# 64 slots for each expert in 32 blocks of two, gathers that leave out empty slots, and the sixth expert's weights loaded during the router

## What is computed

```
h2 = rms_norm(x, norm2_g).reshape(b * s, d)
g_sel = argmax(h2 @ w_rg + b_rg)              # one of 8 groups
top_v, top_i = lax.top_k(e_logits[g_sel], 2)  # 2 of its 8 experts
gate = p_group[:, None] * softmax(top_v)
hid = silu(xb @ w_gate_e[e]) * (xb @ w_up_e[e])
y = hid @ w_down_e[e]                         # for each expert e, its tokens xb
out = x + sum over a token's two experts of gate * y
```

## Time and profile before

| | |
|---|---|
| median of 3 runs | 2459.86 us (2456.59 to 2461.51) |
| profiled execution, its own time | 2460.95 us |
| its span in the profile | 2459.1 us |
| PE busy | 2084.4 us (85%) |
| DVE, ACT, POOL busy | 972.0, 683.7, 169.6 us |
| granted TensorE clock, mean | 0.93 of full speed |
| HBM read and written | 366.62 and 20.48 MB |
| loads of `in_wexp` | 66 of 2048 KB and 66 of 1024 KB |

### The profile page before, as it was taken

The page is one execution under the profiler, slowest core; times in us unless marked ns, Lnnn a source line. Parts: engine busy times, 40 slices in busy tenths (PEclk is TensorE's granted clock), DMA queues, the critical chain, the costliest instruction groups (busy, mean ns, idle before and its releaser), DMA issues.

```text
span 2459.1 us, 22973 instructions
## 1 busy us (share of the span) xinstructions
PE 2084.4 (85%) x9596; PEld 1442.3 (59%) x9596; DVE 972.0 (40%) x1472; ACT 683.7 (28%) x1076; POOL 169.6 (7%) x234
## 2 busy tenths in 40 slices
PE   6999778997999998999998999999946767777752
PEld 5887556887888787777777756666841222222211
DVE  3246443434666524577766255542250000000002
ACT  4233332324444314544444224431110000000000
POOL 1000000002000001010011021100021000000000
PEclk9999888998999999999999999999977888888876
DMA  6432110232322323111210221111276999999934
GB/s 183 137 124 82 43 52 35 103 137 95 103 87 102 137 89 130 69 56 69 73 56 35 99 80 39 48 52 69 112 291 228 425 425 421 411 419 419 418 122 163
DMA packets 51238, 383.34 MB, mean 156 GB/s; under 512 B 7904, under 2 KB 8176, under 8 KB 17984
## 3 DMA queue, kind: packets, MB, share of 16 engines
q1 hardware_dynamic: 38016, 341.33, 35.6%
q0 software_dynamic: 12544, 39.40, 5.1%
q10 hardware_dynamic: 576, 1.16, 0.2%
HBM read 366.62 MB, written 20.48 MB: 157 GB/s over the span
## 4 chain that ended last, share of the span: by engine, by line
PE 70%; DMA 13%; DVE 9%; ACT 4%; issue 2%; POOL 2%; SPq 0%; POOLq 0%; ACTq 0%
PE PS L481 15%; PE PS L482 15%; PE PS L483 15%; DMA AR<-in_wexp 11%; PE PS L958 6%; PE PS L834 4%; PE PS L980 2%; PE PS L528 2%; DVE AR L1174 1%; PE PS L893 1%; DVE rf L990 1%; PE PS L863 1%; ACT rf L1703 1%; DVE AR L1297 1%; DVE AR L1283 1%
## 5 line engine op out<-in xcount | busy, mean ns | idle before, releaser
L481 PE MATMUL PS<-rf,rf 128*128 128x512 f32 (+1 forms) x1896 | 724.2, 382 | 15.2 <-DVE rf L990 8.3
L482 PE MATMUL PS<-rf,rf 128*128 128x512 f32 (+1 forms) x1896 | 712.0, 376 | 0.0
L483 PE MATMUL PS<-rf,rf 128*128 128x512 f32 (+1 forms) x1896 | 711.5, 375 | 0.0
L990 DVE TENSOR_TENSOR rf<-AR,rf 128x1024 fp32r<-128x1024 f32 (+1 forms) x210 | 268.9, 1285 | 437.2 <-ACT rf L1703 437.0
L481 PEld LDWEIGHTS PS<-rf,rf 128*128 128x128 f32 x1896 | 361.0, 190 | 90.5 <-issue 23.1
L483 PEld LDWEIGHTS PS<-rf,rf 128*128 128x128 f32 x1896 | 360.1, 190 | 64.9
L482 PEld LDWEIGHTS PS<-rf,rf 128*128 128x128 f32 x1896 | 360.7, 190 | 63.9 <-issue 2.7
L958 PE MATMUL PS<-AR 128*32 128x512 f32 x1024 | 258.5, 665 | 109.3 <-DMA AR<-in_wexp 97.6
L1703 ACT ACTIVATE rf<-AR 128x1024 fp32r<-128x1024 f32 (+1 forms) x210 | 229.4, 1101 | 382.0 <-PE PS L483 293.6
L958 PEld LDWEIGHTS PS<-AR 128*32 128x32 f32 x1024 | 69.7, 121 | 287.5 <-issue 157.1
L1676 DVE TENSOR_TENSOR AR<-AR,PS 128x256 f32<-128x256 f32 x16 | 6.7, 421 | 370.5 <-ACT AR L2097 370.5
(11 more groups left out here) (328 smaller groups left out, 1890.4 us busy)
## 6 DMA issues: line engine op xcount, KB each, us to landing
AR<-in_wexp SPq DMA_DIRECT2D x66, 2048.0 KB, 24.1
AR<-in_wpack SPq DMA_DIRECT2D x123, 1024.0 KB, 5.0
AR<-in_wexp SPq DMA_DIRECT2D x66, 1024.0 KB, 20.9
AR<-ya POOLq DMA_DIRECT2D x4, 1024.0 KB, 8.0
bvec<-AR POOLq DMA_DIRECT2D x1, 2560.0 KB, 55.7
AR<-in_x SPq DMA_DIRECT2D x4, 512.0 KB, 8.3
AR<-bvec POOLq DMA_DIRECT2D x8, 256.0 KB, 2.9
AR<-in_x POOLq DMA_DIRECT2D x4, 512.0 KB, 5.1
```

Source lines behind the costliest of these rows:

```text
L481: e.i.matmul(o, ws[0], xs[0], start=start, stop=False)
L482: e.i.matmul(o, ws[0], xs[1], start=False, stop=False)
L483: return e.i.matmul(o, ws[1], xs[0], start=False, stop=stop)
L990: e.i.tensor_tensor(rounded(p.place + p.width, p.width), src, rounded(p.place, p.width).bitcast(F32), ALU.subtract).then_inc(*tick("w_lo", ...
```

## The change

`CAP` goes from 32 to 64 and `NOV` from 31 to 15, so a block holds two experts and there are 32 blocks. The two experts of a block are one pair with 64-column stationary operands, and a load waits for the block that used its buffer. On TensorE, VectorE and ScalarE the transposes of block b + 1 move between the gate/up products of block b and the transposes of its hidden rows. The clamp to 511 goes: an empty slot's token is 2048, out of bounds for the gather, and its row is not read. `XR` moves out of `HTo` to the space behind the weights (three rows of tiles) and `GB`, and the sixth expert's weights are loaded with the first five; VectorE now waits for the stores of `h2d` before it writes the masked logits (L1579 before), and ScalarE's squares go to `MGo`. The second and fourth quarters of `oo` lie in another place and wait for the last attention product `ao`.

```diff
@@ -15,8 +15,8 @@
...
-CAP = 32
-NOV = 31
+CAP = 64
+NOV = 15
@@ -169,8 +169,8 @@
...
-        p.place = Fo + 12032 + 4096 * (i % 2)
-        p.free = (read_by(oos[i - 2]) if i > 1 else ("acc", ("so", 7)),)
+        p.place = Fo - 4096 if i % 2 else Fo + 12032
+        p.free = (read_by(oos[i - 2]) if i > 1 else ("acc", ("ao" if i else "so", 7)),)
@@ -407,12 +407,13 @@
...
-        XR, HR = cut(area(HTo, 4096), 4), MG
+        HR = MG
...
+        XR = [area(f + 768 + 1024 * i, 1024) for i in range(3)] + [GB]
@@ -426,13 +427,13 @@
...
-        BEF = area(HTo, 31 * 64).rearrange("p (b e) -> p b e", b=31)
+        BEF = area(GBo, NOV * 64).rearrange("p (b e) -> p b e", b=NOV)
...
+        NBLK = 64 * CAP // 128
...
-        N_PRE = 5
@@ -934,30 +935,35 @@
             m.then_inc(*tick("acc", "rank"))
 
 
-            for blk in range(16):
+            def turned_rows(blk):
                 s = blk % 2
-                xb, xt, hs, hd = XB[:, s, :], cut(XT[:, s, :], 8), HS[:, s, :], cut(HD[:, s, :], 2)
                 e.wait_ge(*at(f"gather{s}", blk))
                 for hf in range(2):
                     b, was = banks.take(("xt", blk, hf), ("a_out" if hf else "v_out", ("xt", blk, hf)))
                     e.wait_ge(*at(*was))
                     for k in range(4):
                         m = e.i.transpose(PS[:, b, 128 * k:128 * k + 128],
-                                          xb[:, 512 * hf + 128 * k:512 * hf + 128 * k + 128], ident)
+                                          XB[:, s, 512 * hf + 128 * k:512 * hf + 128 * k + 128], ident)
                     m.then_inc(*tick("acc", ("xt", blk, hf)))
+
+            turned_rows(0)
+            for blk in range(NBLK):
+                s = blk % 2
+                xt, hs, hd = cut(XT[:, s, :], 8), HS[:, s, :], cut(HD[:, s, :], 2)
                 b, was = banks.take(("gu", blk), ("v_out", ("hm", blk)))
                 e.wait_ge(*at(*was))
                 e.wait_ge(*at("v_out", ("xt", blk, 0)))
                 e.wait_ge(*at("a_out", ("xt", blk, 1)))
-                for pair in range(2):
-                    for k in range(8):
-                        for j in (2 * pair, 2 * pair + 1):
-                            n = 4 * blk + j
-                            e.wait_ge(*at(f"gu{n % 6}", n))
-                            w = cut(area(GUs[n % 6], 4096), 8)
-                            m = e.i.matmul(PS[CAP * j:CAP * j + CAP, b, :], xt[:, k, CAP * j:CAP * j + CAP], w[:, k, :],
-                                           start=k == 0, stop=k == 7)
-                    m.then_inc(*tick("acc", ("gu", blk, pair)))
+                for k in range(8):
+                    for j in range(2):
+                        n = 2 * blk + j
+                        e.wait_ge(*at(f"gu{n % 6}", n))
+                        w = cut(area(GUs[n % 6], 4096), 8)
+                        m = e.i.matmul(PS[CAP * j:CAP * j + CAP, b, :], xt[:, k, CAP * j:CAP * j + CAP], w[:, k, :],
+                                       start=k == 0, stop=k == 7)
+                m.then_inc(*tick("acc", ("gu", blk)))
+                if blk + 1 < NBLK:
+                    turned_rows(blk + 1)
                 b, was = banks.take(("ht", blk), ("v_out", ("hd", blk)))
                 e.wait_ge(*at(*was))
                 e.wait_ge(*at("v_out", ("hm", blk)))
@@ -970,16 +976,15 @@
                     e.wait_ge(*at(*was))
                     b2.append(b)
                 e.wait_ge(*at("v_out", ("hd", blk)))
-                for pair in range(2):
-                    for hf in range(2):
-                        for q in range(2):
-                            for j in (2 * pair, 2 * pair + 1):
-                                n = 4 * blk + j
-                                e.wait_ge(*at(f"dn{n % 6}", n))
-                                w = cut(area(DNs[n % 6], 2048), 2)
-                                m = e.i.matmul(PS[CAP * j:CAP * j + CAP, b2[hf], :], hd[:, q, CAP * j:CAP * j + CAP],
-                                               w[:, q, 512 * hf:512 * hf + 512], start=q == 0, stop=q == 1)
-                    m.then_inc(*tick("acc", ("dn2", blk, pair)))
+                for hf in range(2):
+                    for q in range(2):
+                        for j in range(2):
+                            n = 2 * blk + j
+                            e.wait_ge(*at(f"dn{n % 6}", n))
+                            w = cut(area(DNs[n % 6], 2048), 2)
+                            m = e.i.matmul(PS[CAP * j:CAP * j + CAP, b2[hf], :], hd[:, q, CAP * j:CAP * j + CAP],
+                                           w[:, q, 512 * hf:512 * hf + 512], start=q == 0, stop=q == 1)
+                    m.then_inc(*tick("acc", ("dn2", blk, hf)))
 
 
         def vector(e):
@@ -1529,7 +1534,7 @@
...
-                e.i.scalar_tensor_tensor(out=XR[:, i, :], in0=X[:, i, :], scalar=col("ss3", 4)[:, i:i + 1], in1=GB,
+                e.i.scalar_tensor_tensor(out=XR[i], in0=X[:, i, :], scalar=col("ss3", 4)[:, i:i + 1], in1=GB,
@@ -1575,6 +1580,8 @@
...
+            for i in range(4):
+                e.wait_ge(*at(f"st{i}", "h2"))
@@ -1647,36 +1654,38 @@
...
-            bef = col("bef", 31)
-            for i in range(4):
-                e.wait_ge(*at(f"st{i}", "h2"))
-            e.i.tensor_tensor(BEF, incl.unsqueeze(1).to_broadcast([128, 31, 64]),
-                              cc("iob").unsqueeze(2).to_broadcast([128, 31, 64]), ALU.is_le).then_inc(*tick("v_out", "bef0"))
+            bef = col("bef", NOV)
+            e.i.tensor_tensor(BEF, incl.unsqueeze(1).to_broadcast([128, NOV, 64]),
+                              cc("iob").unsqueeze(2).to_broadcast([128, NOV, 64]), ALU.is_le).then_inc(*tick("v_out", "bef0"))
...
-            e.i.tensor_copy(IA[:, 64:95], bef).then_inc(*tick("v_out", "be0"))
+            e.i.tensor_copy(IA[:, 64:64 + NOV], bef).then_inc(*tick("v_out", "be0"))
...
-            e.i.tensor_scalar(IA[:, 128:175], IA[:, 16:63], 1, None, ALU.logical_shift_right).then_inc(*tick("v_out", "tok0"))
-            e.wait_ge(*at("v_out", "tok0"))
-            e.i.tensor_scalar(IA[:, 128:175], IA[:, 128:175], 511.0, None, ALU.min).then_inc(*tick("v_out", "tok"))
-
-
-            for blk in range(16):
-                s = blk % 2
-                xt, hs, hd, ye = cut(XT[:, s, :], 8), HS[:, s, :], cut(HD[:, s, :], 2), YE[:, s, :]
+            e.i.tensor_scalar(IA[:, 128:175], IA[:, 16:63], 1, None, ALU.logical_shift_right).then_inc(*tick("v_out", "tok"))
+
+
+            def turned_rows(blk):
+                xt = cut(XT[:, blk % 2, :], 8)
...
-                    e.wait_ge(*at("acc", ("gu", blk - 2, 1)))
+                    e.wait_ge(*at("acc", ("gu", blk - 2)))
...
+
+            turned_rows(0)
+            for blk in range(NBLK):
+                s = blk % 2
+                hs, hd, ye = HS[:, s, :], cut(HD[:, s, :], 2), YE[:, s, :]
...
+                if blk + 1 < NBLK:
+                    turned_rows(blk + 1)
...
-                e.wait_ge(*at("acc", ("dn2", blk, 1)))
+                e.wait_ge(*at("acc", ("dn2", blk, 0)))
@@ -2066,7 +2075,7 @@
...
-                e.i.activation(XR[:, i, :], X[:, i, :], ACT.Square, accum_out=col("ss3", 4)[:, i:i + 1]).then_inc(
+                e.i.activation(area(MGo + 1024 * i, 1024), X[:, i, :], ACT.Square, accum_out=col("ss3", 4)[:, i:i + 1]).then_inc(
@@ -2082,19 +2091,24 @@
...
-            for blk in range(16):
+            def turned_rows(blk):
+                xt = cut(XT[:, blk % 2, :], 8)
+                e.wait_ge(*at("acc", ("xt", blk, 1)))
+                if blk > 1:
+                    e.wait_ge(*at("acc", ("gu", blk - 2)))
+                e.i.activation(xt[:, 4:8, :], cut(ps(("xt", blk, 1)), 4), ACT.Copy).then_inc(*tick("a_out", ("xt", blk, 1)))
+
+            e.wait_ge(*at("v_out", "tok"))
+            turned_rows(0)
+            for blk in range(NBLK):
...
-                xt, hs, ye = cut(XT[:, s, :], 8), HS[:, s, :], YE[:, s, :]
-                e.wait_ge(*at("acc", ("xt", blk, 1)))
-                if blk == 0:
-                    e.wait_ge(*at("v_out", "tok"))
-                if blk > 1:
-                    e.wait_ge(*at("acc", ("gu", blk - 2, 1)))
-                e.i.activation(xt[:, 4:8, :], cut(ps(("xt", blk, 1)), 4), ACT.Copy).then_inc(*tick("a_out", ("xt", blk, 1)))
-                e.wait_ge(*at("acc", ("gu", blk, 1)))
+                hs, ye = HS[:, s, :], YE[:, s, :]
+                e.wait_ge(*at("acc", ("gu", blk)))
...
+                if blk + 1 < NBLK:
+                    turned_rows(blk + 1)
@@ -2246,9 +2260,9 @@
...
-            for blk in range(16):
+            for blk in range(NBLK):
...
-                if blk < 15:
+                if blk + 1 < NBLK:
@@ -2287,15 +2301,13 @@
             loads.upto(e, len(chunks))
...
 
-                if n < N_PRE:
+                if n < 6:
                     e.wait_ge(*at("acc", ("oo", 3, 1)))
-                elif n == 5:
-                    e.wait_ge(*at("gather0", 0))
                 else:
```

(20 more changed lines are left out.)

4 lines of the change are left out of this document (2 added, 2 removed).

## The result

| | before | after |
|---|---|---|
| median of 4 runs, us | 2460.69 | 2579.61 |
| lowest and highest, us | 2456.59 to 2462.0 | 2575.27 to 2581.48 |
| the profiled execution, us | 2460.95 | 2575.27 |
| its span, us | 2459.1 | 2573.5 |

The ratio is 1.0484, with an interval of 1.0465 to 1.0502. The forecast of slower was right, and 2609 was 29 us too much.

A forecast was written before the change was run, and what follows sets the result against it. The DMA bounded the experts' stage before; after, a ring of waits through the gather would. T(0) 1880.8 plus 29 x 23.3, then the last blocks and tail, gave span 2607.4, time 2609 us, whole range 2440 to 2680.

The forecast's parts named there:

- The ring: Experts' stage: down products' end, copies, scatter b-1, gather b+1, its transposes, down products of b; 23.3 us per block, chance 0.58.
- formula: Whole kernel: span is 1931.7 + 29 P, and at P = 18.2 the change makes no difference.
- P: Experts' stage: time from one T to the next, forecast 23.3 us for two experts, ends 18.3 and 27.
- T: Experts' stage: the end of a block's down products; from there 1.54 us to the scatter's issue, 1.30 more to the gather's.
- landing of the gather: Experts' stage: gather's issue to its landing among weights, forecast 12.8 us, ends 14.3 and 9.7.
- T(0): First block of the experts' stage: its down products end at 1880.8, from 1875.06 + 5.75.
- Skipped slots: Gathers and scatters: a skipped slot costs nearly what a sent one does, 0.4 us for 75 slots.
- The clock: TensorE in the experts' stage: idling 8 us lowers its clock, costing 1.9 us per block, ends 0 and 4.
- A: Rival, experts' stage: the gather is quick and the DMA stays the bound, 2375 us, faster; chance 0.22.
- B: Rival, experts' stage: the ring is there but short, P 18.3 to 21, 2464 to 2543 us; chance 0.13.
- C: Rival, TensorE: 64-wide matmuls do not overlap, P 27.0, 2716 us; chance 0.05 together with longer rings.
- D: Rival: an overflow round still runs (+35 each) or empty slots still move rows (+20); chance 0.02 on top of the ring.

The follow-up runs named there:

- run 1: Each gather issued one block earlier on POOL, ahead of the scatter it stood behind, against the changed kernel: 2380.14 us, 0.9684 of the kernel before.
- run 2: Transposes of block b+1 put back behind the down products of block b, POOL's order kept, against the changed kernel: 2380.67 us.
- run 3: On POOL, behind the wait for block b's results, gather b+2 issued first and scatter b second, against the changed kernel: 2470.27 us.
- run 12: Weights loaded in pieces of 1024 columns, packets of 4 KB instead of 16 and 8 KB, same bytes and order, against the changed kernel: 2471.81 us.
- run 4: Clamp of empty slots to the last token put back, so each gather sends 128 rows, against the changed kernel: 2618.46 us.
- run 5: Clamp taken away, so empty slots are skipped, nothing else, against the kernel before the change: 2457.52 us, ratio 0.9991.
- run 7: Gather issued one block earlier and the clamp put back (run 1 and run 4 together), against the changed kernel: 2398.28 us.
- run 10: Slot of rank 8a+c sent to partition 8c+a, meant to spread an expert's rows over its 64 partitions, against run 1: 2381.76 us.
- run 9: 68 more transposes that nobody reads on TensorE before the wait for the gather, none in the first and last block, against the changed kernel: 2549.45 us.
- run 8: 48 more identity transposes that nobody reads on TensorE before the wait for the next gather, against the changed kernel: 2584.29 us.
- run 6: Sixth expert's weights loaded only behind the landing of gather 0, as before the change, against run 1: 2378.48 us.

## Why the prediction was right

**The sign and the mechanism.** The ring was written out from the earlier trace rows, before it existed; runs 1 and 2 each open it at one link and take the loss away. The formula's break-even of P = 18.2 stands too: run 3 with 18.65 and run 12 with 18.77 are 11 and 14 us slower than the kernel before beside them, near the 13 and 17 that it gives. Its constant of 1931.7 was a little high: the spans less 29 P give 1921.9 for the change, 1927.2 for run 3 and 1922.9 for run 12.

**Its size.** P was to be 23.3 and is 22.47, term by term:

| term of P | forecast | measured |
|---|---|---|
| T to the scatter, to the gather | 1.54 + 1.30 | 1.47 + 1.30 |
| landing of the gather | 12.8 | 11.9 |
| landing to T, the clock among it | 5.75 + 1.9 | 7.80 (the rest of P) |

The mis-sized term is the landing, 0.9 too long. With the clamp it would have been 12.6 (run 4), not the 13.5 of the earlier trace rows, probably since the DMA now stands idle for part of each block. Skipping took off 0.7, where I had 0.5 and 0.2. Over 29 periods the difference in P is 24 of the 34 us between the forecast span of 2607.4 and 2573.5.

**The start.** T(0) is 1872.3 and not 1880.8. Of the 8.5 us, 5.6 are an offset that is there by 390 us into the span, in code that the change does not touch: the spread of single executions, which my sum took over from the one profiled before. The rest is mostly the first gather (3.4 to land instead of 4.7) and first products a little faster. The end, T(29) to the last store, is 49.7 against 50.9.

**Skipped slots.** "A skipped slot costs nearly what a sent one does" was right for the landing, and run 12 shows why. It had been argued from two scatters without a reason, so part of this was luck. Run 5 extends it to the kernel before (2 us for 4 MB), but run 7 does not fit (18 us for 12.6 MB). The uneven load of run 10 would fit both. If gathers and scatters follow the swizzle that is cited there from the Trainium skill (DMA: Bandwidth & Descriptors, The descriptor swizzle), the eight full engines carry in a block of the kernel before 8 gathered and 8 scattered rows each, clamped or not: no gain. In a block of two they gather 4 of their 8 slots, so the clamp adds 4 packets of 0.16 us (4 KB at a sixteenth of 419 GB/s), 0.64 a block, an estimate of 20 us for 31. That is arithmetic after the fact. The landings go the same way for blocks of two: the late eight of the last load lie 15.8 us behind the others in the mean in run 1 and 10.6 in run 7. But they lie only 3.0 behind in the kernel before and 3.9 in run 5, so less piles up there than such a count of rows would give. No run here evens the load out, and its part in these times stays open.

**The clock.** The forecast took 2.6 us from the earlier trace rows and scaled it down to 1.9. Run 9 shows the same amount by taking it away: the eight transposes take 1.97 in the change and 1.09 there, the down products 4.77 and 3.76 in the mean, together 1.9. Run 8 shows that a shorter idle time doesn't make it smaller in proportion.

**Costs set at nothing.** The sixth expert: nothing (run 6). The stores of `h2d`: the last landed 11.3 us behind its issue, and VectorE did not stand at the logits. No instruction of an overflow round ran. The preload ended near 1840, five us sooner than forecast, which is the offset named above.

**The rivals.** A came to 2375 with a quick gather. The gather is not quick, but where it is hidden (runs 1 and 2) the kernel runs at 2380, so A's price was right and its condition wrong. The rule beside it from the Trainium skill (DMA: Bandwidth & Descriptors, Anatomy of one DMA), an estimate of 2.3 us for 32 rows, is near the transfers that met no weights (at the least 2.6 for a scatter and 3.2 for a gather) and far from those among weights. B is no case of the change, but is what runs 3 and 12 are. C falls: the 32 records of a 64-wide pair's gate/up products take 7.03, as a 32-wide pair's did, and its down products 3.65. D did not occur.

## What to carry to other kernels

When a loop's blocks are made smaller, write out the ring from one block's end to the next, with the loaded latency of each transfer and everything ahead of it in its queue. A latency that was hidden under 32 us may not hide under 16. Here the place of one gather in the issue order was worth 199 us, more than all the rest of the change. The rest took 80 off. The version that beats both kernels is run 1 (or 2): blocks of two, empty slots skipped, and the gather issued before the wait that holds the scatter, at 2380 us, 0.968 of the kernel before.

## What the runs showed of the hardware

- A small indirect transfer beside saturating loads is paid mostly in turns, not in bytes: behind 4.5 us in which none of its packets starts, a scatter and a gather of 128 slots each take 8.3 us against weights in packets of 16 and 8 KB, and 4.5 against packets of 4 KB. The gather lands in 11.9 and in 8.1. Smaller packets for the bulk cost it little: run 12 moved 352 GB/s at a share of 0.93 in 1894 to 2350, run 3, with the same period, 351 at 0.87.
- The second of two indirect transfers lands 2.4 us later, whichever it is (run 3).
- The clock's fall can hit work well after the idle time that caused it: in run 8 the matmuls just behind 3.2 us of idle time ran at 1.00, and those two us later at 0.50.
- Where the loads of weights are the bound, eight of a load's sixteen landings fall behind the other eight, by 15.8 us in the mean at the end of run 1. In its last 24 us of loads the DMA share falls from 0.48 to 0.10; in run 10 it stays near 0.5 for 16 us. Rows packed at the front of each 64 slots are a candidate; no run shows the cause.
